# First chunks of five projections computed tile by tile together

## What is computed

```python
def hybrid_layer(x, ...):
    proj = rmsnorm(x, norm_mix_g) @ w_in
    mixed = gates0 * (attn @ w_branch_attn) + gates1 * (pooled @ w_branch_pool)
    x = x + mixed @ w_out                          # first output
    up = conv(rmsnorm(x, norm_ffn_g) @ w_up)       # feed-forward
    return x + (silu(gate) * val) @ w_down

def second_block(x, c, ...):
    mod = silu(c) @ ada_w + ada_b                  # modulation
    p = modulate(rmsnorm(x), mod) @ w_in_2         # mixer
    x = x + gt_mix * (concat([y_conv, y_rwkv]) @ w_out_2)       # second output
    u = modulate(rmsnorm(x), mod)
    q = u @ peer_w_q                               # query
    return rmsnorm(x + gt_ffn * peer_ffn(u, q, sub_keys, expert_u, expert_v))
```

## Time and profile before

| | us |
|---|---|
| median of 3 runs | 1415.87 |
| lowest, highest | 1413.18, 1418.66 |
| the profiled execution's own time | 1418.13 |
| its span (first to last instruction) | 1416.3 |
| PE busy | 1387.7 |
| DVE busy | 998.1 |
| ACT busy | 819.6 |
| POOL busy | 386.3 |

### The profile page before, as it was taken

How to read it: one execution, slowest core, us unless ns; L and a number is a source line. 1 busy time by engine, 2 the same in 40 slices (tenths; PEclk the granted TensorE clock), 3 DMA queues, 4 the chain that set the end, 5 groups by cost and what they waited for, 6 DMA issues and landing times.

```text
span 1416.3 us, 31065 instructions
## 1 busy us (share of the span) xinstructions
PE 1387.7 (98%) x11588; PEld 1296.2 (92%) x11588; DVE 998.1 (70%) x1821; ACT 819.6 (58%) x1572; POOL 386.3 (27%) x205
## 2 busy tenths in 40 slices
PE   8999999999999998999999999999999999999998
PEld 8989989999979987999999999999998888888887
DVE  5478757878777686679956878888855555555554
ACT  6454656656557893445444567777765555555553
POOL 0620000000000691077883047777750000000000
PEclk9999999999999998999999999999999999999998
DMA  8456466667734201554555554444455565655551
GB/s 286 171 206 243 161 243 238 245 229 263 266 114 151 96 4 32 179 172 166 185 180 189 174 173 157 157 156 157 155 195 197 194 191 193 193 193 193 193 192 62
DMA packets 70754, 252.97 MB, mean 179 GB/s; under 512 B 7664, under 2 KB 9968, under 8 KB 70128
## 3 DMA queue, kind: packets, MB, share of 16 engines
q1 hardware_dynamic: 69488, 245.40, 51.4%
q10 hardware_dynamic: 1152, 5.98, 1.2%
HBM read 249.25 MB, written 2.10 MB: 177 GB/s over the span
## 4 chain that ended last, share of the span: by engine, by line
PE 90%; DVE 5%; ACT 2%; issue 2%; DMA 1%; SPq 0%; POOL 0%; DVEq 0%; ACTq 0%
PE bank L2440 24%; PE bank L1836 19%; PE bank L1837 18%; PE bank L1838 18%; PE bank L2241 1%; PE bank L2405 1%; PE bank L2406 1%; ACT w_hi L565 1%; PE bank L2452 1%; DVE arena L1066 1%; DVE w_lo L1044 1%; DMA raw<-in_w_in 1%; ACT arena L847 1%; PE bank L2389 1%; PE bank L1886 0%
## 5 line engine op out<-in xcount | busy, mean ns | idle before, releaser
L1836 PE MATMUL bank<-x_pair,w_hi 128*128 128x256 f32 x2120 | 613.4, 289 | 7.6 <-DVE x_pair L1088 2.5
L1837 PE MATMUL bank<-x_pair,w_hi 128*128 128x256 f32 x2120 | 599.9, 283 | 0.0
L1838 PE MATMUL bank<-x_pair,w_lo 128*128 128x256 f32 x2120 | 599.6, 283 | 0.0
L565 ACT ACTIVATE w_hi<-raw 128x1024 fp32r<-128x1024 f32 x416 | 438.0, 1053 | 189.7 <-PE bank L2440 166.8
L1044 DVE TENSOR_TENSOR w_lo<-raw,w_hi 128x1024 fp32r<-128x1024 f32 x297 | 368.1, 1241 | 220.4 <-ACT w_hi L565 218.6
L1836 PEld LDWEIGHTS bank<-x_pair,w_hi 128*128 128x128 f32 x2120 | 406.5, 192 | 15.3 <-issue 4.8
L1837 PEld LDWEIGHTS bank<-x_pair,w_hi 128*128 128x128 f32 x2120 | 406.7, 192 | 0.3
L1838 PEld LDWEIGHTS bank<-x_pair,w_lo 128*128 128x128 f32 x2120 | 406.5, 192 | 0.0
L1752 POOL TENSOR_TENSOR w_lo<-raw,w_hi 128x1024 fp32r<-128x1024 f32 x119 | 285.9, 2403 | 214.2 <-ACT w_hi L565 140.2
L2440 PE MATMUL bank<-w_hi,x_pair 128*128 128x512 f32 x984 | 263.1, 389 | 0.0
L2440 PEld LDWEIGHTS bank<-w_hi,x_pair 128*128 128x128 f32 x984 | 184.7, 188 | 38.3
(11 more groups left out here) (347 smaller groups left out, 1540.4 us busy)
## 6 DMA issues: line engine op xcount, KB each, us to landing
raw<-in_u SPq DMA_DIRECT2D x128, 512.0 KB, 3.3
raw<-in_v SPq DMA_DIRECT2D x128, 512.0 KB, 4.3
raw<-in_w_in SPq DMA_DIRECT2D x54, 512.0 KB, 4.3
arena<-in_ada SPq DMA_DIRECT2D x48, 512.0 KB, 4.6
raw<-in_w_up SPq DMA_DIRECT2D x44, 512.0 KB, 4.8
raw<-in_w_down SPq DMA_DIRECT2D x22, 512.0 KB, 3.3
raw<-in_w_out SPq DMA_DIRECT2D x16, 512.0 KB, 3.5
raw<-in_w_q SPq DMA_DIRECT2D x16, 512.0 KB, 3.2
```

Of the source, the lines that this page charges most:

```text
L565: act.activation(w_hi[:, s], raw[:, s], ACT.Copy).then_inc(hi_ready, 1)
L1836: pe.matmul(o, w, xh, start=start, stop=False, skip_group_check=True)
L1837: pe.matmul(o, w, xl, start=False, stop=False, skip_group_check=True)
L1838: return pe.matmul(o, wl, xh, start=False, stop=stop_, skip_group_check=True)
```

## The change

`reduce_fresh` takes a number of chunks and computes that many in step: for each activation tile the three matmuls of every chunk, each chunk in its own bank. It waits first until the lower halves of all its chunks are made. It takes 1 chunk at the input projection, as before; 2 at feed-forward, mixer and second output; 4 at first output and query. Beside that: some modulation pieces move behind the first chunks of feed-forward and mixer; the mixer's first `keep_busy` grows from 3 to 5; in the first output PE's sums of squares start two tiles later; in the query `score(0)` moves from behind chunk 2 to behind chunk 4; at the mixer's start ACT waits for 3 signals instead of 4, and DVE's `modulation_rows` and a memset move behind the second `shift`; in the second output DVE makes the lower halves of the convolution's tiles between the two halves of the other branch.

```diff
-            act.wait_ge(S("pads_zero"), 4)
+            act.wait_ge(S("pads_zero"), 3)
...
             split(MIX - 1 + AHEAD)
-            modulation_rows(ADA // KT - 1)
             dve.tensor_scalar(keep_mu, V("rwkv_mu_2", 14), -1.0, 1.0, ALU.mult, ALU.add).then_inc(S("pads_zero"), 1)
-            dve.memset(cy[:, :, 0:30], 0.0).then_inc(S("pads_zero"), 1)
...
                 if n == 1:
+                    modulation_rows(ADA // KT - 1)
+                    own.mark(dve.memset(cy[:, :, 0:30], 0.0))
+                if n == 3:
                     modulation_cols(ADA // KT - 1)
...
                 dve.tensor_tensor(yf[:, v], yf[:, v], bon[:, v], ALU.add).then_inc(S("y_done"), 1)
-            for f in range(4):
-                dve.wait_ge(S("mixed_hi"), KT + f + 1)
-                dve.tensor_tensor(x_lo[:, f], co[:, f], x_hi[:, f].bitcast(F32), ALU.subtract).then_inc(S("mixed_lo"), 1)
+                conv_low(2 * f)
+                conv_low(2 * f + 1)
...
-            def reduce_fresh(b, o, ready, before=0):
+            def reduce_fresh(b, ready, before=0, chunks=2):
-                s = b % RING
-                pe.wait_ge(lo_ready, b + 1)
+                pe.wait_ge(lo_ready, b + chunks)
                 for k in range(KT):
                     pe.wait_ge(S(ready), before + k + 1)
                     c = slice(k * P, k * P + P)
-                    m = three(o, w_hi[:, s, c], w_lo[:, s, c], x_hi[:, k], x_lo[:, k], k == 0, k == KT - 1)
-                m.then_inc(chunk_used, 1)
+                    for n in range(chunks):
+                        s = (b + n) % RING
+                        m = three(bank[n][:, 0:TOK], w_hi[:, s, c], w_lo[:, s, c], x_hi[:, k], x_lo[:, k], k == 0, k == KT - 1)
+                        if k == KT - 1:
+                            m.then_inc(chunk_used, 1)
...
-            reduce_fresh(W_OUT, bank[0][:, 0:TOK], "mixed_lo")
-            for k in range(1, KT):
+            reduce_fresh(W_OUT, "mixed_lo", 0, 4)
+            for k in range(4, KT):
                 if k >= 4:
                     pe.wait_ge(S("x_added"), k - 3)
                 reduce(W_OUT + k, bank[k % 4][:, 0:TOK])
-                if k >= 2:
-                    sum_squares(1, k - 2, sq)
+                sum_squares(1, k - 4, sq)
+            sum_squares(1, KT - 4, sq)
+            sum_squares(1, KT - 3, sq)
...
-            modulation(ADA_EARLY + 3, ADA_EARLY + 8)
-            reduce_fresh(FFN, bank[0][:, 0:TOK], "norm_lo", KT)
-            reduce(FFN + 1, bank[1][:, 0:TOK])
+            modulation(ADA_EARLY + 3, ADA_EARLY + 5)
+            reduce_fresh(FFN, "norm_lo", KT)
+            modulation(ADA_EARLY + 5, ADA_EARLY + 8)
...
-            modulation(ADA - 2, ADA)
-            keep_busy(1, 3)
-            reduce_fresh(MIX, bank[0][:, 0:TOK], "norm_lo", 2 * KT)
-            reduce(MIX + 1, bank[1][:, 0:TOK])
+            modulation(ADA - 2, ADA - 1)
+            keep_busy(1, 5)
+            reduce_fresh(MIX, "norm_lo", 2 * KT)
+            modulation(ADA - 1, ADA)
...
-            mix(2, 3)
+            mix(2, 4)
             modulation_turn(ADA // KT - 1)
-            mix(3, 7)
+            mix(4, 7)
...
-            reduce_fresh(W_OUT2, bank[0][:, 0:TOK], "mixed_lo", KT)
-            for k in range(1, KT):
+            reduce_fresh(W_OUT2, "mixed_lo", KT)
+            for k in range(2, KT):
...
-            reduce_fresh(W_Q, bank[0][:, 0:TOK], "norm_lo", 3 * KT)
+            reduce_fresh(W_Q, "norm_lo", 3 * KT, 4)
...
-            for j in range(1, 16):
-                if j >= 4:
-                    pe.wait_ge(S("q_taken"), j - 3)
+            for j in range(4, 16):
+                pe.wait_ge(S("q_taken"), j - 3)
                 reduce(W_Q + j, bank[j % 4][:, 0:TOK])
-                if j >= 2 and j % 2 == 0:
+                if j == 4:
+                    score(0)
+                if j % 2 == 0:
                     score(j // 2 - 1)
```

More of the change, by code:

```diff
@@ L1533, in _, with conv_low @@
             own.wait()
+            def conv_low(f):
+                dve.wait_ge(S("mixed_hi"), KT + f + 1)
+                dve.tensor_tensor(x_lo[:, f], co[:, f], x_hi[:, f].bitcast(F32), ALU.subtract).then_inc(S("mixed_lo"), 1)
             for f in range(2):
@@ L1933, in _ @@
                 pe.matmul(bank[6][:, 0:TOK], mixb[:, 0, 0:P], mixb[:, 0], start=True, stop=True)
-            reduce_fresh(0, bank[0][:, 0:TOK], "norm_lo")
+            reduce_fresh(0, "norm_lo", 0, 1)
             def score(h):
```

## The result

The changed kernel takes 1446.86 us (median of 4 runs, 1445.59 to 1448.38); the kernel before, run beside it, 1415.96 (4 runs, 1413.18 to 1418.66). The ratio is 1.0214, 95% interval 1.0201 to 1.0226: slower by 2.1%, about 30 us. The profiled execution's own time is 1446.95, its span 1445.2, against 1418.13 and 1416.3 before: +28.8 in own time, +28.9 in the span. PE's mean granted clock went from 0.989 to 0.982.

A forecast was written before the change was run, and what follows sets the result against it. PE was taken to bound the kernel almost everywhere (98% of span). Terms 10.8 + 1.6 - 0.4 + 0.8 - 1.0 + 0.6 + 10.2 + 3.2 = 25.8 us gave 1443.9 profiled, 1441.6 by the median; range 1430 to 1452.

The forecast's parts named there:

- First output, 10.8: First output: PE waits until 176.0 for the fourth chunk's lower half; first residual add, and all behind it, 10.8 us later.
- The clock: 5.6 foreseen: Half-clock stretches after PE's stands: 1.6 us at first output, 0.8 after its adds, 3.2 in the query.
- the ring: First output: upper half on ACT, lower half on DVE, add, square on ACT; adds 2.99 us apart, so delay stays.
- The upper bound of 11.2: All stands of PE: twice the foreseen slow-clock loss, 11.2 us in all.
- Query, 10.2: Query: PE waits for POOL's lower halves, before chunk 4 and for `score(1)`; block of `score(2)` 10.2 us later, without clock.
- Mixer, -1.0: Mixer start: ACT skips waits for copy and memset, fewer tile waits; gain 1.0 us, between 0.5 and 1.5.
- Second output, +0.6: Second output: PE's 0.46 us wait goes, but chunk 0 completes later, delaying first add; loss 0.6 us, -0.5 to 1.
- feed-forward, -0.4: Feed-forward: two chunks per tile remove PE's stalls, partly offset by moved modulation pieces; gain 0.4 us, between 0 and 1.
- the gates don't bind: PE's `lo_ready` wait ahead of both four-chunk blocks: lower halves ready in time, not slower; 1421 us, chance 0.06.
- a gate is paid back: Late first output or query made good by slack in the stage behind; half the sum, +12, 1428 us; chance 0.06.
- the clock stays low for longer: Each stand leads to several slow stretches, ACT and PE keep waiting past `score(2)`; +35, 1451 us; chance 0.06.
- interleaving halves the clock: All interleaved blocks, 336 matmuls, run at half clock, 40 us more; 1482 us; chance 0.01.

The follow-up runs named there:

- the gate alone: Kernel before, one chunk after another, but PE waits for four chunks' lower halves ahead of first output's and query's first chunk; 1431.47 us, ratio 1.0094.
- late squares alone: Kernel before, with only ACT's order in both output loops changed: it squares each residual tile one step later; 1415.61 us, ratio 0.9988.
- The fastest kernel: Changed kernel with two chunks in all five places and ACT squaring each tile one step later in both outputs; 1409.42 us, ratio 0.9954.

## Why the prediction was right

Predicted 1441.6 (1430 to 1452), measured 1446.86; in the profiled execution's own time a sum of +25.8 against +28.8. Its terms:

- **First output, 10.8.** Right, in place and mechanism. The lower half that PE waits for ends at 175.35, which is the foreseen 176.0 moved by the 0.64 us that this execution was ahead. The wait is 8.28 us against "about 8", and the first add is 13.3 us later against 10.8 and a slow stretch; with the stand filled it was 10.9. (The prediction's own terms, 186.6 less 175.91, make 10.7.) The adds keep their 2.99 us, so that the delay stays. Beside the order, the run with the gate alone shows how it splits.
- **The clock: 5.6 foreseen, about 8.8 measured. This is the step that failed in size.** The prediction took one stretch of 3.1 us at 0.50 for each stand, "1.6 here, 0.8 after the ring, 3.2 in the query". Behind the 8.28 us stand PE worked 5.6 us at 0.50: 26 matmuls, where 5.6 us at full clock hold 47, so 21 x 0.12 = 2.5 us lost, and not 1.6. (At 0.50 the starts are 0.21 us apart, so such work loses 0.44 of its time rather than half.) After the ring the norm lost 1.8. In the query there were three stretches, not two, since the wait of 1.91 us at `score(1)`, which the prediction had foreseen as a wait of 2 us, was given no stretch of its own; filling the stands gave 4.5 us back there. 2.5 + 1.8 + 4.5 = 8.8. The step behind these sizes, one stretch of one length for each stand of 2 us or more and none for shorter ones, isn't what the runs show: the 2.19 us wait of the first output was followed by none, and the last section has shorter waits that were. The upper bound of 11.2 held it.
- **Query, 10.2.** Right: with the stands filled the block of `score(2)` was 10.7 us late. Each foreseen wait is there: 6.78 us for POOL (7 foreseen), 2.94 before chunk 4 (3), 1.91 at `score(1)` (2).
- **Mixer, -1.0.** ACT's first drain is 9.04 us behind the norm (430.04 - 421.00), 9.76 before (416.07 - 406.31), so 0.7 earlier as foreseen; PE's third chunk came 0.7 us earlier against the norm too. A little high.
- **Second output, +0.6, and feed-forward, -0.4.** The second output's mechanism is right: its block began 12.4 us later than before (565.68 and 578.06), its first add 13.65, so the way from block to first add grew by 1.3 us against 1.1 foreseen, and DVE waited 0.62 us for PE there. Yet nothing was lost against the mixer's norm, which had moved by 14.7: PE came to this block 2.3 us earlier against it. 0.7 of that is the mixer's start and some 0.5 PE's wait, which is gone; the other 1.1 isn't traced, and PE's slow stretches lie at other places there. Feed-forward gained nothing where 0.4 was foreseen: its stage is 0.2 us longer.
- **The rivals.** That the gates don't bind is out by the 8.28 and 6.78 us. That a gate is paid back is out by the two runs that undo one stage: 0.96 and 1.14% add up. That the clock stays low for longer was right in direction: 3.2 us, where that rival had 9 (35 - 25.8). That interleaving halves the clock is out: from 181 to 189, in the midst of the four-bank block, 69 matmuls touch 8 us at clock 1.00. The Trainium skill (TensorE: Matmul & The Clock Gate, section "A second HAM failure mode: psum-queue depth-cycling") reports a clock that swings for one bf16 kernel that cycles through PSUM banks; it doesn't say that every such order runs at half clock, as the prediction read it. The trace shows no such swing in this block.

The sum of the measured terms closes, up to the block of `score(2)`: 25.8 foreseen + 3.2 more clock + 0.5 (the query's waits, 10.7 for 10.2) + 0.6 (feed-forward) - 0.6 (mixer and second output together) + 0.3 (from the second output to the query's norm) - 0.6 (this execution's earlier start) = 29.2, which is how much later that block starts. The span is 28.9 longer.

## What to carry over

To compute several output tiles in step saves PE waits on late activations, but it makes all of them wait for the last weight tile and makes the first result as late as the last: price both, at the consumer of the first result, before the fan-out is chosen. Behind such a block look at which ring sets the pace of the results; if that isn't PE, the time that PE saves comes back as a stand and a slow clock, as with two chunks alone, and the edit of the ring is needed with it. A filler in the stand bought back the clock here (8.5 us), not the wait (10.9 and 10.7 us stayed).

## What had not been expected

- After a long stand the slow stretch is not only that behind it. The clock read 0.50 from 171 on, 4.3 us of them idle, and then 5.6 us at work: some 10 us in one piece. In the query the three waits were followed by 3.3, 3.2 and 3.2 us of work at 0.50, but by 5.9, 5.4 and 3.6 us in the run with the first output undone, where they were 7.11, 2.94 and 1.91 us long. Behind a stand of 1.33 us (two chunks) it was 3.2 us, and behind the 1.1 us waits of the earlier trace rows none. So the length of a stand doesn't give the cost by itself.
- **Equal code doesn't always get an equal clock.** The wait of 2.19 us before chunk 4 of the first output left the clock at 1.00 in the changed kernel, and was followed by 0.50 in the one with fillers. The two waits of 1.1 us left it at 1.00 in the kernel before, and the second of the same two was followed by 0.50 in the run with two chunks in three stages. The kernel before has such work even behind a wait of 0.68 us that ended at 592.54. Windows of PE in these three, in this order:

```profile
190.80:194.20 3.40, 3.40 (x18) 0.51 0.94 340
```

```profile
172.50:175.40 2.90, 2.90 (x13) 0.50 0.00 0
```

```profile
594.40:597.60 3.20, 3.20 (x11) 0.50 0.73 310
```

  The stand near 490 in the kernel before was followed by 0.50. With the late squares alone, where the code between mixer norm and second output is the same, it wasn't (windows of PE):

```profile
489.35:493.35 4.00, 3.41 (x112) 1.00 0.01 4
...
533.35:537.35 4.00, 3.51 (x66) 0.57 0.00 0
```

  A second such place lies near 535; in a third, near 557, PE works 6.5 us at 0.50 in the kernel before and 3.3 us in the two others. The fastest kernel's profile has neither of the first two, and its way from mixer norm to second output is 160.3 us long; 162.4 with late squares alone, where the second came, 163.9 in the kernel before, where both came. So 3.6 of the 9 us by which its profile is shorter are not shown to be the edit's, and single profiles are compared stage by stage here, with their clock, not by their ends. What decides whether the clock falls there stays open.
